# Attention layers, experts' selections and the x norm in a new order, and the mixer's output projection by token tiles

## The chip, the core and the metric

The kernel runs on one core of one Trainium2 chip. That core has a matrix engine (PE, TensorE), a vector engine (DVE), a scalar engine (ACT), GpSimd (POOL), a queue engine that issues the transfers (SP), and 16 DMA engines between memory and the on-chip buffer. Each engine runs its own list of instructions in order; they meet only at semaphores. The metric is the device time of one execution in microseconds (us), the median of several runs.

## What is computed

Two transformer blocks stand one behind the other on 256 tokens of width 1024, all in float32. The parts that matter here, cut from the reference:

```python
for i in range(DEPTH):                       # first_block: two layers
    h = rmsnorm(x, attn_norm[i]); proj = h @ w_in[i]
    ...                                      # dilated attention oa, windowed attention ob
    mix = jnp.concatenate([rmsnorm(merge_heads(oa), mix_norm_a[i]),
                           rmsnorm(merge_heads(ob), mix_norm_b[i])], axis=-1)
    x = x + mix @ w_out[i]
    ...                                      # layer 0: swiglu; layer 1: moe_swiglu, 8 experts, top 2
return rmsnorm(x, final_norm)

def ffn_half(s, shift, scale, gate, g_pre, g_post, w_in, w_out):      # second block
    h = swiglu_2(modulate(rmsnorm_2(s, g_pre), shift, scale), w_in, w_out)
    return s + 0.5 * gate * rmsnorm_2(h, g_post)
def token_mixer(...):
    ...
    return (g_hy * y_hy + g_da * y_da) @ w_o
```

The second block runs `ffn_half` on a context and on x, then the mixer (a long convolution and a differential attention), then another `ffn_half`.

## The kernel before

The tokens are two tiles (`tt`) of 128. A float32 operand of a large product is split into a high part (rounded to the fast format fp32r) and a low remainder, and a product is three matmuls, high by high, high by low and low by high. ACT makes every high part (a copy that rounds), DVE every low part (a subtraction); PE waits for both. A weight block is 1024 x 512 values and comes in two halves `h` of four 128-row chunks, so one half for one tile is 12 matmuls of 512 columns, and one block for one tile is two halves. `weight_high` and `weight_low` (L1588, L2255), or `A_parts` in the feed-forward phases (L1604, L2287), make the parts; the blocks lie in a ring of two (`ringA`), which SP refills as soon as a half has been used.

The order of work is written out by hand, engine by engine; no scheduler moves anything.

**Attention layers** (`heads` on PE, L1043, and its counterparts on ACT and DVE). 16 heads go through in four groups `g`. For each, PE turns the softmax weights (`turn_weights`, L1078), ACT copies heads 0 and 2 (L1890) and DVE heads 1 and 3 (L2620) back to memory, PE multiplies by the values (`values`, L1088 to L1090) and DVE normalises into `O` (`outputs`, L2625). Between these, PE works off rows of a modulation matrix (`mods`, L1038, `spreads`, L1020). The output goes through an rms norm in two halves: columns 0 to 511 (groups 0 and 1) and 512 to 1023 (groups 2 and 3). A half's norm is squares (`tile_stats`, L1565) and a square root (`tile_root`, L1569) on ACT, a scaling on DVE (`tile_scale`, L2236), transposes on PE (`turn_rows`, L736), a high part on ACT (`rows_high`, L1578) and a low part on DVE (`rows_low`, L2252). The first half's norm starts behind group 2. Then `project_split` (L763) multiplies by `w_out`: for block 0 tile 0 half 0, tile 0 half 1, tile 1 half 0, tile 1 half 1, and so on. Exponentials and square roots need different tables on ACT, so a table load stands at L1569.

**Experts.** Each of the eight experts works on at most 128 gathered tokens in 14 steps `n` (`expert`, L976 on PE, L1758 on ACT, L2408 on DVE). A step on PE is half a gate or up block (L903), two transposes (L918), the other half, and 12 matmuls of the down projection (L933), which wait for `hds`, the transposed activations split by ACT (L1704) and DVE (`part_low`, L2351). The result of expert e-1 is scattered behind steps 2 and 3 of expert e (L973), and DVE adds it to x (`add`, L2400). DVE also makes the selection matrices (`one_hot`, L2375): the gated one of e and the plain one of e+1, both behind step 3. Experts 1 to 6 are one hardware loop; inside an expert the first `head` pairs of steps are written out and the rest is a loop (`blocks`, L465).

**The norm of x behind the experts** stands within the first steps of the context's feed-forward phase `ff0c` (`x_rows`, L1972 on ACT, L2780 on DVE): the squares, a root, DVE's scaling by `final_norm`, squares and roots again (L1565), and another scaling (L2236). All of it stands in ACT's and DVE's lists ahead of `hidden` of step 1 (L1634, L2305), for which PE's down projection of step 0 waits (L858).

**The mixer's output projection `wo`** (L1303) is two blocks `n` for two tiles, eight half blocks. PE takes them as (n, h, tile) 000, 001, 010, 011, 100, 110, 101, 111. A tile is complete once both of its blocks are. Then come per tile the squares (L2151, L2159) and the root (L2160) on ACT, DVE's scaling and addition to x (`mixed_out`, `mixed_add`, L3021, L3026), and the norm for the last feed-forward phase `ff1` (L1565, L2236), which PE turns (L736) and multiplies (L806).

## Time and profile before

| | us |
|---|---|
| median of 3 runs | 2653.58 |
| the runs | 2653.3, 2653.58, 2659.06 |
| profiled execution, its own time | 2659.7 |
| its span, first to last instruction | 2657.9 |

PE is busy for 96% of the span, DVE for 68%, ACT for 55%; the mean granted clock of PE is 0.978 of full speed. A row of a timeline reads: start in us, duration in us, engine, line, operation, tile written and tiles read, shapes, number of instructions merged, and in brackets how long the engine sat idle before it and what ended that. "issue" stands there where the profile names no releaser.

### The profile page before, as it was taken

The page shows a single profiled execution, that of the slowest core. Times are in us where ns is not written, and L with a number is a line of the kernel's source. Part 1 is how long each engine was busy: PE and PEld are TensorE (multiplying, and loading weights), DVE is VectorE, ACT ScalarE, POOL GpSimd, SP SyncE. Part 2 cuts the span into 40 slices and gives each one's busy share as a digit, 9 for nine tenths or more (in the row PEclk, how much of TensorE's full clock was granted, in tenths as well). Part 3 has the DMA queues.
Part 4 walks back from the last instruction along what each step waited for, and adds up shares of the span by engine and source line. Part 5 has one row for each costly group of instructions (what it writes and reads, how often), then busy time and mean ns, then how long its engine had stood idle before and what let it go on. Part 6 is the DMA issues. An engine that isn't in the chain of part 4 may idle for free.

```text
span 2657.9 us, 33567 instructions
## 1 busy us (share of the span) xinstructions
PE 2548.6 (96%) x11951; PEld 2023.4 (76%) x11951; DVE 1814.3 (68%) x1779; ACT 1452.1 (55%) x1613; POOL 54.4 (2%) x40
## 2 busy tenths in 40 slices
PE   7899999889999999999999998999999999998998
PEld 6578887667878788888878786888884688776787
DVE  6464446558898888888888985645444475776544
ACT  4454444547777777776767774435432343465443
POOL 0000000010000000000000000500000000000000
PEclk9899999889999999999999999999999999998999
DMA  6865552659999999999999995755544244435551
GB/s 216 297 207 189 189 174 90 243 174 374 351 353 348 354 342 347 356 351 342 360 328 372 327 341 203 227 191 183 187 145 130 85 143 131 129 107 173 193 185 68
DMA packets 327743, 631.65 MB, mean 238 GB/s; under 512 B 14089, under 2 KB 112937, under 8 KB 327465
## 3 DMA queue, kind: packets, MB, share of 16 engines
q1 hardware_dynamic: 326792, 627.35, 68.0%
q0 software_dynamic: 864, 3.15, 0.4%
q8 instruction: 55, 0.90, 0.1%
q14 instruction: 32, 0.25, 0.0%
HBM read 629.40 MB, written 1.05 MB: 237 GB/s over the span
## 4 chain that ended last, share of the span: by engine, by line
PE 85%; DVE 7%; ACT 4%; issue 3%; DMA 1%; SPq 0%; DVEq 0%; ACTq 0%
PE ps L829 19%; PE ps L903 19%; PE ps L933 11%; PE ps L858 10%; PE ps L1303 6%; PE ps L763 5%; PE ps L1330 2%; PE ps L1235 1%; DVE As L2290 1%; PE ps L1038 1%; PE ps L958 1%; PE ps L918 1%; PE ps L842 1%; ACT Bs L1724 1%; ACT As L1694 1%
## 5 line engine op out<-in xcount | busy, mean ns | idle before, releaser
L2290 DVE TENSOR_TENSOR As<-ringA,As 128x2048 fp32r<-128x2048 f32 x318 | 730.9, 2300 | 227.4 <-ACT As L1613 131.9
L903 PE MATMUL ps<-As,xgs 128*128 128x512 f32 x2688 | 660.7, 395 | 5.7 <-DVE As L2290 3.0
L903 PEld LDWEIGHTS ps<-As,xgs 128*128 128x128 f32 x2688 | 494.8, 188 | 112.3 <-issue 5.8
L1694 ACT ACTIVATE As<-ringA 128x2048 fp32r<-128x2048 f32 x224 | 428.8, 1914 | 28.3 <-PE ps L903 28.1
L829 PE MATMUL ps<-As,xs 128*128 128x512 f32 x1456 | 376.1, 396 | 3.9 <-DVE hh L2325 3.9
L933 PE MATMUL ps<-Bs,hds 128*128 128x512 f32 x1332 | 322.4, 391 | 11.8 <-DVE hds L2351 9.0
L829 PEld LDWEIGHTS ps<-As,xs 128*128 128x128 f32 x1456 | 271.9, 189 | 63.3 <-DVE hh L2325 4.8
L933 PEld LDWEIGHTS ps<-Bs,hds 128*128 128x128 f32 x1332 | 248.6, 188 | 69.9 <-issue 16.5
L2370 DVE TENSOR_TENSOR Bs<-ringB,Bs 128x2048 fp32r<-128x2048 f32 x111 | 254.1, 2290 | 12.4 <-ACT Bs L1724 10.8
L858 PE MATMUL ps<-Bs,hds 128*128 128x512 f32 x1056 | 250.6, 393 | 4.1 <-issue 4.1
L1724 ACT ACTIVATE Bs<-ringB 128x2048 fp32r<-128x2048 f32 x111 | 213.1, 1920 | 69.4 <-PE ps L933 69.4
L858 PEld LDWEIGHTS ps<-Bs,hds 128*128 128x128 f32 x1056 | 199.9, 190 | 47.0 <-issue 4.5
L1613 ACT ACTIVATE As<-ringA 128x2048 fp32r<-128x2048 f32 x94 | 179.8, 1913 | 29.1 <-PE ps L829 12.8
L2334 DVE TENSOR_TENSOR Bs<-ringB,Bs 128x2048 fp32r<-128x2048 f32 x44 | 103.7, 2358 | 118.1 <-ACT Bs L1667 118.1
L1667 ACT ACTIVATE Bs<-ringB 128x2048 fp32r<-128x2048 f32 x44 | 84.3, 1915 | 136.5 <-PE ps L858 136.5
L2260 DVE TENSOR_TENSOR ringL<-ringA,ringH 128x2048 fp32r<-128x2048 f32 x42 | 96.1, 2290 | 56.5 <-ACT ringH L1593 56.3
L1704 ACT ACTIVATE hds<-ps 128x256 fp32r<-128x256 f32 x112 | 43.2, 385 | 153.9 <-PE ps L918 151.3
L763 PE MATMUL ps<-As,xs 128*128 128x512 f32 (+1 forms) x384 | 117.7, 390 | 7.8 <-DVE ringL L2260 5.7
L1634 ACT ACTIVATE hds<-ps 128x256 fp32r<-128x256 f32 x94 | 31.3, 382 | 169.8 <-PE ps L842 161.7
L1593 ACT ACTIVATE ringH<-ringA 128x2048 fp32r<-128x2048 f32 x42 | 80.2, 1911 | 79.2 <-PE ps L1303 57.6
L829 PE MATMUL ps<-As,xnR 128*128 128x512 f32 x352 | 112.8, 402 | 1.8 <-issue 1.8
L1655 ACT ACTIVATE sg<-ps 128x256 f32<-128x256 f32 x94 | 36.1, 385 | 125.9 <-PE ps L829 124.8
(390 smaller groups left out, 3300.3 us busy)
## 6 DMA issues: line engine op xcount, KB each, us to landing
ringA<-in_moe_w_gate SPq DMA_DIRECT2D x112, 1024.0 KB, 5.2
ringA<-in_moe_w_up SPq DMA_DIRECT2D x112, 1024.0 KB, 5.6
ringB<-in_moe_w_down SPq DMA_DIRECT2D x112, 1024.0 KB, 5.6
ringA<-in_w_ff_in SPq DMA_DIRECT2D x132, 512.0 KB, 4.7
ringA<-in_w_in SPq DMA_DIRECT2D x56, 1024.0 KB, 5.3
ringA<-in_w_ada SPq DMA_DIRECT2D x36, 1024.0 KB, 5.8
ringB<-in_w_ff_out SPq DMA_DIRECT2D x33, 1024.0 KB, 5.0
ringA<-in_dense_w_gate SPq DMA_DIRECT2D x28, 512.0 KB, 3.6
```

The costliest lines, as they stand in the source:

```text
L763: m = mm(ps[:, 4 + 2 * (n % 2) + tt, 0:cols], xs[:, l, k, tt * P:(tt + 1) * P], w, start=k == 0 and m_ == 0, stop=k == KC - 1 and m_ == 2)
L829: m = mm(ps[:, bank, :], lhs(l, tt, k), As[:, h, r, k % 4, :], start=k == 0 and n == 0, stop=k == KC - 1 and n == 2)
L858: m = mm(ps[:, 4 + 2 * tt + half, :], hds[:, buf, l, q, :], w[:, half * 512:(half + 1) * 512], start=first and q == 0 and n == 0, stop=q = ...
L903: m = mm(ps[:, bank, :], lhs(l, tt, k), As[:, h, r, k % 4, :], start=k == 0 and n == 0, stop=k == KC - 1 and n == 2)
L933: m = mm(ps[:, 4 + 2 * tt + half, :], hds[:, u if T == 1 else tt, l, q, :], (Bs[:, q, r, :] if weights is None else weights[r][:, q, :])[: ...
L1303: m = mm(dst, lhs[l][:, k, tt * P:(tt + 1) * P], w[q], start=k == 0 and m_ == 0, stop=k == KC - 1 and m_ == 2)
L1613: A(As[:, h, 0, :, :], ringA[:, (p["a"] + u) % 2, 4 * h:4 * h + 4, :], ACT.Copy).then_inc(A_high, 1)
L1694: A(As[:, h, 0, :, :], ringA[:, (p["a"] + u) % 2, 4 * h:4 * h + 4, :], ACT.Copy).then_inc(A_high, 1)
L1724: A(Bs[:, :, 0, :] if dst is None else dst, ringB[:, b0 % 2, :, :], ACT.Copy).then_inc(B_high, 1)
L2290: V.tensor_tensor(As[:, h, 1, :, :], ringA[:, (p["a"] + u) % 2, 4 * h:4 * h + 4, :], f32(As[:, h, 0, :, :]), ALU.subtract).then_inc(A_spli ...
L2334: V.tensor_tensor(Bs[:, :, 1, :], ringB[:, (p["b"] + u) % 2, :, :], f32(Bs[:, :, 0, :]), ALU.subtract).then_inc(B_low, 1)
L2370: V.tensor_tensor(lo, ringB[:, (p["b"] + u) % 2, :, :], f32(hi), ALU.subtract).then_inc(B_low, 1)
```

## The change

It reorders instructions; the arithmetic stays. In four places:

1. **Attention layers.** ACT takes the squares of the first half of the norm ahead of the last modulation row of group 2, loads the square root's table between its two copies of group 3, and takes the root behind them. DVE scales that half behind its copies of group 3 instead of behind group 2. PE takes `values(3)` and `mods(8)` ahead of the first half's transposes. ACT makes the high part of weight half 0 ahead of the squares of the second half, and that of half 1 behind the last `spreads`; DVE takes the low part of the first half's rows behind the scaling of the second.
2. **Experts**, on DVE alone: the second `add` moves behind `part_low` of step 4, the gated `one_hot` behind step 4 and the plain one behind step 5; three pairs of steps are written out instead of two.
3. **The x norm**: the second squares and roots, the table load and the second scaling move behind `hidden` of step 1, by a new hook `within`.
4. **`wo`**: the half blocks go 000, 001, 010, 100, 110, 011, 101, 111, so tile 0 is complete after five of them. ACT's statistics follow that order, and weight half 1 of `ff1` is split behind tile 0's rows instead of ahead. The added 1 in `TILES_THROUGH` makes SP's load of that half wait for the sixth half block, where it waited for the fourth.

```diff
+        TILES_THROUGH[ph["wo"]["a"]] += 1
...
                     if g == 3:
+                        values(g)
+                        mods(8)
                         pe.wait_ge(nm_ready, 4 * (l + 1))
                         for tt in range(TILES):
                             turn_rows(f"mix{l}", tt, 0)
-                        values(g)
-                        mods(8)
                         spreads(8)
                         continue
...
-            for n in range(2):
-                for h, tt in ((0, 0), (0, 1), (1, 0), (1, 1)) if n == 0 else ((0, 0), (1, 0), (0, 1), (1, 1)):
...
+            for n, h, tt in ((0, 0, 0), (0, 0, 1), (0, 1, 0), (1, 0, 0), (1, 1, 0), (0, 1, 1), (1, 0, 1), (1, 1, 1)):
+                if tt == 0:
...
                         before(2 * i + u)
                     if not (leads and isinstance(i, int) and i == 0 and u == 0):
                         hidden(*((i, 0) if u else (i - 1, 1)))
+                    if within and isinstance(i, int):
+                        within(2 * i + u)
...
                         if j == 0:
+                            if g == 3:
+                                nc.scalar.preload_act_table(ACT.Sqrt)
                             spreads(2 * g + 1)
+                    if g == 2:
+                        for tt in range(TILES):
+                            tile_stats(f"mix{l}", tt, O, [(o_done, 4 * l + 2)], slice(0, D // 2), tt)
                     if g < 3:
                         mods(2 * g + 2)
                         exponentials(g + 1, (0, 1))
                         spreads(2 * g + 2)
                         exponentials(g + 1, (2, 3))
                         mods(2 * g + 3)
-                    if g == 2:
-                        for tt in range(TILES):
-                            tile_stats(f"mix{l}", tt, O, [(o_done, 4 * l + 2)], slice(0, D // 2), tt)
-                        tile_root(0, 2, D // 2)
+                tile_root(0, 2, D // 2)
...
                 p = ph[f"out{l}"]
+                weight_high(p, 0, 0)
+                for tt in range(TILES):
+                    tile_stats(mix, tt, O, [(o_done, 4 * (l + 1))], slice(D // 2, D), 2 + tt)
+                mods(8)
+                tile_root(2, 4, D // 2)
                 for tt in range(TILES):
                     rows_high(mix, tt, 0, mixc)
-                for h in range(2):
-                    weight_high(p, 0, h)
-                mods(8)
-                for tt in range(TILES):
-                    tile_stats(mix, tt, O, [(o_done, 4 * (l + 1))], slice(D // 2, D), 2 + tt)
-                tile_root(2, 4, D // 2)
                 spreads(8)
+                weight_high(p, 0, 1)
                 for tt in range(TILES):
                     rows_high(mix, tt, 1, mixc)
...
                 if n == 1:
                     act.wait_ge(x_ready, XR["moe"])
                     squares(lambda tt: x[:, tt, :], 1, 1e-5, lambda tt, q: x_tok[:, tt, :])
-                    for tt in range(TILES):
-                        tile_stats("ff0x", tt, x, [(x_ready, XR["final"])])
-                        tile_root(tt, tt + 1, D, 1e-6)
-                    nc.scalar.preload_act_table(ACT.Silu)
 
+            def x_stats(n):
+
+                if n == 1:
+                    for tt in range(TILES):
+                        tile_stats("ff0x", tt, x, [(x_ready, XR["final"])])
+                        tile_root(tt, tt + 1, D, 1e-6)
+                    nc.scalar.preload_act_table(ACT.Silu)
+
...
-            for tt in range(TILES):
-                act.wait_ge(tile_done, p["td"] + tt + 1)
+            def mixed_first(tt):
+
+                act.wait_ge(tile_done, p["td"] + 2 * tt + 1)
...
-            for h in range(2):
-                A_parts(ph["ff1"], 0, 0, 0, h, fresh=True)
 
             def mixed_root(tt):
 
-                act.wait_ge(tile_done, p["td"] + 2 + tt + 1)
+                act.wait_ge(tile_done, p["td"] + 2 * tt + 2)
...
+            mixed_first(0)
+            A_parts(ph["ff1"], 0, 0, 0, 0, fresh=True)
             mixed_root(0)
+            mixed_first(1)
             tile_stats("ff1", 0, x, [(x_mixed, 1)])
             tile_root(0, 1, D, 1e-6)
             mixed_root(1)
             split_rows(0)
+            A_parts(ph["ff1"], 0, 0, 0, 1, fresh=True)
             tile_stats("ff1", 1, x, [(x_mixed, 2)])
             tile_root(1, 2, D, 1e-6)
             split_rows(1)
...
-                    if n in (2, 3) and not first:
-                        add(e - 1, n - 2)
-                    if n == 3:
+                    if n == 2 and not first:
+                        add(e - 1, 0)
+                    if n == 4:
                         if not first:
                             dve.wait_ge(selg_tp, e)
                         one_hot(e, 2 * e + 2, True)
-                        if not final:
-                            dve.wait_ge(gathered, 2 * e + 2)
-                            one_hot(e + 1, 2 * e + 3, False)
+                    if n == 5 and not final:
+                        dve.wait_ge(gathered, 2 * e + 2)
+                        one_hot(e + 1, 2 * e + 3, False)
...
                     if not lead:
                         part_low(e, i - 1, u, 1)
+                    if isinstance(i, int) and i == 2 and u == 0 and not first:
+                        add(e - 1, 1)
...
-                blocks(dve, NB1, body, 2)
+                blocks(dve, NB1, body, 3)
...
                     if g == 3:
                         for tt in range(TILES):
-                            rows_low(mix, tt, 0, mixc)
+                            tile_scale(mix, tt, O, 1, lower, tt)
                     outputs(g)
-                    if g == 2:
-                        for tt in range(TILES):
-                            tile_scale(mix, tt, O, 1, lower, tt)
                 weight_low(p, 0, 0)
                 for tt in range(TILES):
                     tile_scale(mix, tt, O, 2, upper, 2 + tt)
+                for tt in range(TILES):
+                    rows_low(mix, tt, 0, mixc)
                 weight_low(p, 0, 1)
                 for tt in range(TILES):
                     rows_low(mix, tt, 1, mixc)
...
                     last.then_inc(x_ready, 1)
-                    dve.wait_ge(x_ready, XR["final"])
-                    for tt in range(TILES):
-                        tile_scale("ff0x", tt, x, tt + 1)
+            def x_scale(n):
+
+                if n == 1:
+                    dve.wait_ge(x_ready, XR["final"])
+                    for tt in range(TILES):
+                        tile_scale("ff0x", tt, x, tt + 1)
+
...
             mixed_out(0)
             mixed_add(0)
-            A_parts(ph["ff1"], 0, 0, 0, 1)
             tile_scale("ff1", 0, x, 1)
             plain_rows(0)
             mixed_out(1)
             split_rows(0)
             mixed_add(1)
+            A_parts(ph["ff1"], 0, 0, 0, 1)
             tile_scale("ff1", 1, x, 2)
             plain_rows(1)
             split_rows(1)
```

DVE's feed has the same `within` hook behind its `hidden`.

What stands on **ACT at the end of the attention of layer 1**, from the squares of the norm's first half on. `arena` holds the softmax weights and `O`, `xn` the normed rows, `xs` the split rows, `As` the high part of the weights, `arow` a modulation row. Before:

```order
L1565 ACTIVATE xn,ss<-arena 128x512 [waits o_done]
L1565 ACTIVATE xn,ss<-arena 128x512 [waits o_done,act_step]
L1569 ACT_TABLE_LOAD
L1569 ACTIVATE std<-ss,small 128x2 [waits act_step]
L1890 ACTIVATE arena<-ps 128x384 [waits pt_done] x2
L1578 ACTIVATE xs<-ps,vcol 128x128 [waits pn_tp]
L1578 ACTIVATE xs<-ps,vcol 128x128 x3
L1578 ACTIVATE xs<-ps,vcol 128x128 [waits pn_tp]
L1578 ACTIVATE xs<-ps,vcol 128x128 x3
L1593 ACTIVATE As<-ringA 128x2048 [waits A_full00]
L1593 ACTIVATE As<-ringA 128x2048 [waits A_full01]
L1684 ACTIVATE arow<-ps 128x512 [waits spread,tile_done]
```

And now (the squares of the first half stand further up):

```order
L1892 ACTIVATE arena<-ps 128x384 [waits pt_done]
L1895 ACT_TABLE_LOAD
L1892 ACTIVATE arena<-ps 128x384 [waits pt_done]
L1569 ACTIVATE std<-ss,small 128x2
L1593 ACTIVATE As<-ringA 128x2048 [waits A_full00]
L1565 ACTIVATE xn,ss<-arena 128x512 [waits o_done]
L1565 ACTIVATE xn,ss<-arena 128x512 [waits o_done,act_step]
L1686 ACTIVATE arow<-ps 128x512 [waits spread,tile_done,act_step]
L1569 ACTIVATE std<-ss,small 128x2
L1578 ACTIVATE xs<-ps,vcol 128x128 [waits pn_tp]
L1578 ACTIVATE xs<-ps,vcol 128x128 x3
```

The first copy of group 3 no longer stands behind squares, table load and root, and the first half's rows stand behind the second half's squares.

**DVE in steps 3 and 4 of an expert of the loop**, from the low part of the down weights (`Bs`) of step 3 on; `hds` is what PE's down projection waits for. Before:

```order
L2370 TENSOR_TENSOR Bs<-ringB,Bs 128x2x1024 [waits B_high]
L2398 REGISTER_ALU
L2400 TENSOR_TENSOR x<-x,ps 128x1024 [waits mixed_back]
L2379 ISA [waits selg_tp,added]
L2379 COPY small<-slots 128x2
L2380 REGISTER_ALU
L2380 COPY small<-gates 128x2
L2381 REGISTER_ALU
L2384 TENSOR_SCALAR arena<-c,small 128x128 [waits col_ready]
L2384 TENSOR_SCALAR arena<-c,small 128x128
```

And now:

```order
L2384 TENSOR_TENSOR Bs<-ringB,Bs 128x2x1024 [waits B_high]
L2364 REGISTER_ALU
L2365 TENSOR_TENSOR hds<-ps,hds 128x256 [waits hd_high]
L2412 REGISTER_ALU
L2414 TENSOR_TENSOR x<-x,ps 128x1024 [waits mixed_back]
L2301 REGISTER_ALU [waits added]
L2302 TENSOR_TENSOR As<-ringA,As 128x2048 [waits A_high]
L2301 REGISTER_ALU
L2302 TENSOR_TENSOR As<-ringA,As 128x2048 [waits A_high]
L2382 REGISTER_ALU
L2384 TENSOR_TENSOR Bs<-ringB,Bs 128x2x1024 [waits B_high]
L2393 ISA [waits selg_tp]
```

`hds` of step 4 stands directly behind step 3, and the addition and the selections behind it.

**ACT behind `wo`**, from its first statistics on (`fnrow` takes squares nobody reads, `std` the root). Before:

```order
L2151 ACTIVATE fnrow,ss<-ps 128x512 [waits tile_done]
L2152 ACTIVATE std<-ss,small 128x1 [waits act_step]
L2151 ACTIVATE fnrow,ss<-ps 128x512 [waits tile_done,act_step]
L2152 ACTIVATE std<-ss,small 128x1 [waits act_step]
L1613 ACTIVATE As<-ringA 128x2048 [waits A_full00,act_step]
L1613 ACTIVATE As<-ringA 128x2048 [waits A_full01]
L2159 ACTIVATE fnrow,ss<-ps 128x512 [waits tile_done]
L2160 ACTIVATE std<-ss,std 128x1 [waits act_step]
```

And now:

```order
L2161 ACTIVATE fnrow,ss<-ps 128x512 [waits tile_done]
L2162 ACTIVATE std<-ss,small 128x1 [waits act_step]
L1613 ACTIVATE As<-ringA 128x2048 [waits A_full00,act_step]
L2167 ACTIVATE fnrow,ss<-ps 128x512 [waits tile_done]
L2168 ACTIVATE std<-ss,std 128x1 [waits act_step]
L2161 ACTIVATE fnrow,ss<-ps 128x512 [waits tile_done]
L2162 ACTIVATE std<-ss,small 128x1 [waits act_step]
```

Tile 0's root no longer stands behind tile 1's first squares and the second half of `As`.

## Rows read from the trace of the kernel before

**Rows 1.** Waits of PE: engine, line, releaser, us in total, times, longest.
```profile
PE ps L933 <- DVE hds L2351: 9.3, 16, 1.1
...
PE ps L1078 <- ACT arena L1890: 4.9, 3, 2.4
```

**Rows 2.** Busy time by stretch: window, length, PE, PEld, DVE, ACT, POOL, PEclk, DMA, GB/s.
```profile
147.50:157.00 9.50, 9.50 (x43) 7.71 (x42) 6.50 (x9) 3.54 (x2) 0.00 (x0) 1.00 0.08 19
...
521.50:528.40 6.90, 6.90 (x34) 6.79 (x32) 2.72 (x9) 5.75 (x10) 0.00 (x0) 0.50 0.00 0
```

**Rows 3.** Timeline of PE, end of the attention of layer 0, then of layer 1.
```profile
137.39 0.39 PE L1090 MATMUL ps<-arena 128*128 128x64 f32 x2
137.61 0.39 PE L1088 MATMUL ps<-arena 128*128 128x64 f32 x2
...
149.10 0.63 PE L763 MATMUL ps<-As,xs 128*128 128x512 f32 x2
...
519.11 0.87 PE L1078 MATMUL ps<-c,arena 128*128 128x128 f32 x3 [2.19 <-ACT arena L1890]
...
540.85 0.63 PE L763 MATMUL ps<-As,xs 128*128 128x512 f32 x2
```

**Rows 4.** Timelines of ACT and of DVE in layer 1, the same place.
```profile
517.00 1.28 ACT L1569 ACT_TABLE_LOAD   x1
518.29 0.30 ACT L1569 ACTIVATE std<-ss,small 128x2 f32<-128x2 f32 x1
...
522.65 2.18 ACT L1578 ACTIVATE xs<-ps,vcol 128x128 fp32r<-128x128 f32 x8 [2.14 <-PE ps L736]
524.67 3.76 ACT L1593 ACTIVATE As<-ringA 128x2048 fp32r<-128x2048 f32 x2
...
537.86 2.15 DVE L2252 SCALAR_TENSOR_TENSOR xs<-ps,vcol,xs 128x128 fp32r<-128x128 f32 x8
```

**Rows 5.** Timelines of PE and DVE in steps 3 and 4 of expert 1.
```profile
758.94 3.03 PE L933 MATMUL ps<-Bs,hds 128*128 128x512 f32 x12 [1.08 <-DVE hds L2351]
...
755.47 1.21 DVE L2400 TENSOR_TENSOR x<-x,ps 128x1024 f32<-128x1024 f32 x1
...
758.33 0.42 DVE L2351 TENSOR_TENSOR hds<-ps,hds 128x256 fp32r<-128x256 f32 x1
758.67 4.49 DVE L2290 TENSOR_TENSOR As<-ringA,As 128x2048 fp32r<-128x2048 f32 x2
```

**Rows 6.** Busy time by stretch (columns as in rows 2): experts 1 to 6.
```profile
700.00:1470.00 770.00, 760.92 (x3518) 622.98 (x3517) 679.63 (x488) 545.83 (x402) 0.00 (x0) 1.00 0.97 350
```

**Rows 7.** DMA queues within 842:1472, experts 2 to 6: packets, MB, share.
```profile
q1 hardware_dynamic: 92960, 220.21, 96.4%
```

**Rows 8.** Timelines of PE and DVE at the x norm, first steps of `ff0c`.
```profile
1639.94 8.46 PE L858 MATMUL ps<-Bs,hds 128*128 128x512 f32 x24 [4.07 <-issue]
1648.24 1.04 PE L736 MATMUL ps<-c,arena 128*128 128x128 f32 x8
...
1632.32 2.48 DVE L2786 SCALAR_TENSOR_TENSOR x<-x,rr,fnrow 128x1024 f32<-128x1024 f32 x2
...
1639.41 0.76 DVE L2305 TENSOR_TENSOR hds<-ps,hds 128x256 fp32r<-128x256 f32 x2 [0.74 <-ACT hds L1634]
1641.48 2.29 DVE L2290 TENSOR_TENSOR As<-ringA,As 128x2048 fp32r<-128x2048 f32 x1 [1.32 <-ACT As L1613]
```

**Rows 9.** Timelines of PE, ACT and DVE behind `wo`.
```profile
2451.88 1.97 PE L736 MATMUL ps<-c,xn 128*128 128x128 f32 x8 [3.11 <-DVE xn L2236]
2456.99 5.13 PE L806 MATMUL ps<-As,xs 128*128 128x512 f32 x12 [3.14 <-DVE xs L3042]
...
2465.99 5.78 PE L806 MATMUL ps<-As,xs 128*128 128x512 f32 x24 [0.22 <-DVE xs L3042]
...
2444.67 0.58 ACT L2159 ACTIVATE fnrow<-ps 128x512 f32<-128x512 f32 x1
...
2440.63 2.29 DVE L2290 TENSOR_TENSOR As<-ringA,As 128x2048 fp32r<-128x2048 f32 x1 [4.25 <-ACT As L1613]
```

More of the change, by code:

```diff
@@ L1461, in _ @@
             free, p = p["jd"], ph["wo"]
-            for n in range(2):
-                for h, tt in ((0, 0), (0, 1), (1, 0), (1, 1)) if n == 0 else ((0, 0), (1, 0), (0, 1), (1, 1)):
-                    if tt == 0:
-                        weights_split(p, n, h)
-                    if n == 0:
-                        pe.wait_ge(ot_lo, 4 + 2 * h + tt + 1)
-                    if h == 0:
-                        pe.wait_ge(pj_dve, free + 2 * n + tt + 1)
-                    m = products(p, n, h, ps[:, 4 + 2 * n + tt, :], tt, split_h)
-                    if h:
-                        m.then_inc(tile_done, 1)
-                    elif tt == TILES - 1:
-                        m.then_inc(A_lo_free, 1)
-                    if n == 0 and h == 0 and tt == 0:
-                        pe.wait_ge(y_mixed, 4)
-                        turn_out(YH, 4, 1)
+            for n, h, tt in ((0, 0, 0), (0, 0, 1), (0, 1, 0), (1, 0, 0), (1, 1, 0), (0, 1, 1), (1, 0, 1), (1, 1, 1)):
+                if tt == 0:
+                    weights_split(p, n, h)
+                if n == 0:
+                    pe.wait_ge(ot_lo, 4 + 2 * h + tt + 1)
+                if h == 0:
+                    pe.wait_ge(pj_dve, free + 2 * n + tt + 1)
+                m = products(p, n, h, ps[:, 4 + 2 * n + tt, :], tt, split_h)
+                if h:
+                    m.then_inc(tile_done, 1)
+                elif tt == TILES - 1:
+                    m.then_inc(A_lo_free, 1)
+                if n == 0 and h == 0 and tt == 0:
+                    pe.wait_ge(y_mixed, 4)
+                    turn_out(YH, 4, 1)
             for hf in range(2):
@@ L1623, in x_parts, with feed @@
                     A(xs[:, 0, 4 * h:4 * h + 4, :], src[:, 4 * h:4 * h + 4, :], ACT.Copy).then_inc(high, 1)
-            def feed(p, T, e=0, ahead=False, head=1, leads=True, drains=True, before=None, split_rows=None):
+            def feed(p, T, e=0, ahead=False, head=1, leads=True, drains=True, before=None, within=None, split_rows=None):
                 nb = p["nb"]
@@ L1999, in context_end @@
                     stats(call["mixc"], [(x_ready, XR["ff0c"])], lambda tt: cs[:, tt, :], eps=1e-6)
-            feed(ph["ff0c"], 2, ahead=True, head=2, drains=False, before=x_rows)
+            feed(ph["ff0c"], 2, ahead=True, head=2, drains=False, before=x_rows, within=x_stats)
             feed(ph["ff0x"], 2, head=2, leads=False, before=context_end)
@@ L2295, in x_parts, with feed @@
                     x_low(src, done, h, high, split)
-            def feed(p, T, e=0, ahead=False, head=1, leads=True, drains=True, after=None, split_rows=None, settles=True):
+            def feed(p, T, e=0, ahead=False, head=1, leads=True, drains=True, after=None, within=None, split_rows=None, settles=True):
                 nb = p["nb"]
@@ L2309, in body @@
                         hidden(*((i, 0) if u else (i - 1, 1)))
+                    if within and isinstance(i, int):
+                        within(2 * i + u)
                     nxt = (i + 1, 0) if u else (i, 1)
@@ L2808, in context_end @@
                     scaled("mixc", cs)
-            feed(ph["ff0c"], 2, ahead=True, head=2, drains=False, after=x_rows)
+            feed(ph["ff0c"], 2, ahead=True, head=2, drains=False, after=x_rows, within=x_scale)
             feed(ph["ff0x"], 2, head=2, leads=False, after=context_end)
```

## The prediction

> **What bounds the kernel now.** The page shows PE as the engine that is nearly always at work; in the six experts from 700 to 1470 us it is busy for 760.92 of 770 us [rows 6]. The time is PE's work plus the gaps in it, and this change touches no matmul, so I read first the list of what PE waited for and then, gap by gap, the timelines of PE and of the engine named. Three places stand out. PE waits 9.3 us in 16 pieces for the split `hds` of the experts, made by DVE, and 4.9 us in 3 pieces for ACT's copies of the turned softmax weights [rows 1]. At the end of layer 1 the second of three groups of turns starts 2.19 us late, because ACT loads a table (517.00) and takes a root ahead of its first copy [rows 3, 4]. Behind the experts PE stands still for 4.07 us and then runs 24 matmuls in 8.46 us [rows 8]; behind `wo` it stands still for 3.11 and 3.14 us [rows 9]. Not every wait leaves PE at the same speed: the stretch behind the late turns of layer 1 has a granted clock of 0.50, the lower of the two levels, 1.2 GHz, while in layer 0 the stretch from 147.50 on has 1.00, 2.4 GHz [rows 2].
>
> **Attention layers.** I count each up to the first matmul of the second half of `w_out` for tile 0, the 13th of the projection; it is the second of the row at 540.85, at 541.08, and in layer 0 at 149.33 [rows 3]. Behind it nothing changes its place. Layer 1, after the change: PE is free to turn at 519.11 - 2.19 = 516.92. ACT's first copy then takes half a us (519.11 less the root's end, 518.59, is 0.52) to 517.4, the load 1.28 to 518.7 [rows 4], the second copy to 519.2. The values that need it (10 or 11 pairs at 0.22 us as in layer 0 [rows 3]) take 2.4 us, to 521.6. Then comes what is now in a row: DVE's two `outputs` (0.8), ACT's squares of the second half (1.5), the modulation row (0.5) and root (0.3), all estimates by the like pieces in front of 517.00, and the first half's high and low rows, each eight in 2.2 [rows 4], of which tile 0's four are needed. The projection starts at about 527.1. Its 12 matmuls end at 529.9. Here the order brings a **new wait**: the second half's weight is split only behind the rows: 1.9 high (half of 3.76) [rows 4], 2.3 low (as in [rows 9]), and tile 0's second rows 1.1 (half of 2.15) [rows 4]. That makes the 13th matmul start at 532.35, after a wait of 2.4. Gain 541.08 - 532.35 = 8.7. Against it stands the clock: if the new wait leaves PE at the low level for its next eight matmuls, each costs 0.2 more, 1.7 together; I take 7.0. At worst, if the low level of this stretch stays whatever the waits, I put it at 3.4, since then mostly the waits go and PE's own work is the limit. The same chain laid on layer 0, whose PE was mostly fast already, gives 143.45 for 149.33: 5.9, less the same 1.7, so some 4.5 with the bounds 3 and 5.9.
>
> The median run was 6 us shorter than the profiled one. I assume that part of this is the long slow stretch of layer 1 [rows 2] and credit layer 1 with 5.3 rather than 7.0 against the median.
>
> As to the table load, the row is 517.00 plus 1.28, and the root starts at 518.29 [rows 4]: the load costs its own 1.28 us and nothing behind it. The Trainium skill, "ScalarE: Activation LUTs", section "What ACT_TABLE_LOAD costs", adds a drain of about 1.38 us to each switch, about 2.66 in all. By that rule the second copy would come 1.4 us later in each layer and the sum would be 2.8 smaller; the trace does not show the drain, so I leave it out.
>
> **Experts.** Before, DVE goes from the low part of the down weights straight to the addition (755.47), then the two selections, then `hds` (758.33), and PE waits 1.08 us for it at 758.94 [rows 5]. After, `hds` follows the weights at about 755.9, two us before PE is free at 757.86: that wait goes. It occurs once in each of experts 1 to 6 with about 1.07, in expert 0 with 0.55 and in expert 7 with 0.20, together 7.2. The rest of the 9.3 [rows 1] are waits of 0.2 to 0.3 in steps 0 and 2, which nothing moves. What is late next is DVE itself: the 1.21 of addition [rows 5] and 0.8 of the gated selection now stand ahead of the next `hds`. Worked forward (addition to 757.3, two `As` of 4.49 together which wait for ACT, to 762.7, `Bs` 2.3 to 765.2, selection to 765.95) this is ready about 0.45 before PE is free at 766.4; the step behind it, with the plain selection, keeps 0.55. Over the stretch DVE is busy 679.63 of 770 us [rows 6], so there is room on average. If both margins are overestimated by 0.5 us at each expert, some 3 of the 7.2 return: 4 to 8.3 is my range, the upper end being every piece of step 3 and 2 gone.
>
> **The x norm.** Now the second squares and roots, a table load and DVE's second scaling stand ahead of `hidden`, whose low part ends at 1640.1 [rows 8]; after, ACT's copy can start behind the first root, and DVE's `hds` stands directly behind its scaling, done at 1634.80 [rows 8], before PE ends the previous step at 1639.94 - 4.07 = 1635.87. The 4.07 goes, and the 24 matmuls should take 5.6 instead of 8.46, since they no longer follow a pause. PE is through them at 1641.5 and through the turns (1.04) at 1642.5. What is late next is the split of block 2: ACT's work adds up to the same, less the 0.55 of the copy that now goes first, so its low part at DVE, 1641.48 plus 2.29 [rows 8], ends at about 1643.2. Before, the gate matmuls followed the turns at 1649.03. Gain 5.8; bounds 3 (the 24 still slow) and 6.9.
>
> **`wo`.** PE ends `wo` at 2451.88 - 3.11 = 2448.77. Tile 0 was complete two half blocks before that and is now complete three before, 36 matmuls of 0.24 us, at 2440.15. Its last squares started at 2444.67, behind the second half of `As` [rows 9]. Now DVE limits: ACT makes the first half of `As` without tile 1's squares ahead of it, 1.0 sooner, so its low part, which followed ACT at 2440.63 for 2.29, ends at 2441.9. Scaling (1.6), addition (1.25), squares (1.25), root (0.3) and scaling (0.9), estimates by the instructions of like shape, end at 2447.1, before PE is done. So its 3.11 wait goes; the 3.14 behind the turns stays, since high and low rows are as long as before. The eight turns may take 1.04 as in [rows 8] instead of 1.97 [rows 9]. The feed starts at 2452.7 instead of 2456.99, and tile 1's, before at 2465.99 [rows 9], at 2461.6 or so. Gain 4.2, bounds 2.5 and 4.5. The second half of the weight, loaded two half blocks later, lands about 2448 and is split by 2455.4, about when it is needed; this is the thinnest cover of this part.
>
> **Sum.** Against the profiled run of 2659.7: 4.5 + 7.0 + 7.2 + 5.8 + 4.2 = 28.7, so 2631.0. Against the median of 2653.58, with 5.3 for layer 1: 27.0, so 2626.5.
>
> **Rivals.**
> (a) DVE becomes the bound in the experts and the waits return two steps later: then the change does not do there what it says. For it: margins of half a us, and more work in a row on an engine that is 88% busy [rows 6]. Against: the average room of 90 us. Gain 21, **2632.5**. Chance 0.14.
> (b) The lower clock level stays in the layers whatever the order, for PE is fully busy at 0.50 from 521.50 [rows 2]; the parts there give 4 together, perhaps one late load besides: **2634**. Chance 0.15.
> (c) The new wait costs only itself, and no low level follows: 3.4 to 5 more, **2622**. For it: 1.00 from 147.50 on in layer 0, where PE had waited shortly before [rows 2]. Chance 0.11.
> (d) Slower: the new wait of 2.4 us stands *inside* the projection, and PE falls to the low level there. If it stayed low for all 96 matmuls of each projection, it would cost 0.2 x 96 x 2 = 38 and give **2665**. It decides against the change only if the low level outlasts some 70 matmuls of each; rows 2 show a fall lasting in layer 1 and none in layer 0. Chance 0.04.
> (e) DVE's loop body in the experts grows by the written-out pair, from 122 to 141 instructions. In 630 us of five experts only the data queue appears [rows 7], no fetch of instructions, so I put no price on a jump back. With 15 us of DVE idle per expert (90 over 6) [rows 6] a stall of 1 us per jump would be hidden, and one of 3 us where DVE has half a us of room would cost 2.5 at 5 jumps, 12 in all: **2639**. Chance 0.02. The Trainium skill, "Runtime: NRT & Kernel Launch", section "Instruction fetch mechanics", says that a taken branch to a target outside the window held stalls for a fetch; a longer body would make that likelier. No row here shows such a stall.
>
> **How the numbers follow.** The forecast has 0.54; its own range is 2622 to 2631. (a), (b) and most of (c) lie within 2618 to 2637, which is what I give: the summed lower bounds (3, 3.4, 4, 3, 2.5, together 16) would give 2637.7, the upper ones (5.9, 8.7, 8.3, 6.9, 4.5, together 34) 2619. A measurement tells 0.2%, or 5.3 us, from no change. Faster by more than that are the forecast, (a), (b), (c) and (e), 0.96 together, less 0.02 for parts failing together: 0.94. Within it 0.02, slower (d) 0.04.
>
> **What would show it.** Right: no wait at the second turns of group 3, a wait of about 2.4 us at the 13th matmul of each projection; the wait for `hds` down from 9.3 us to about 2; no idle time ahead of the 24 matmuls of `ff0c` and 5.6 us for them; one wait of 3 us behind `wo` instead of two. Wrong: waits for `hds` at steps 5 and 6 of the experts (a), a clock of 0.50 through the projections (b, d), a late second half of `ff1`'s weights.

## The result, and the profile after

The changed kernel takes 2629.09 us (median of four executions, 2618.15 to 2629.64). The kernel before takes 2655.76 (median of four, 2653.3 to 2659.06). The ratio is 0.9887, with a 95% interval of 0.9868 to 0.9905. Beside other kernels it was timed once more, with six executions: 2628.49 us, ratio 0.9895 [0.9877, 0.9913]. The forecast was 2626.5 us, in a range of 2618 to 2637.

Page of the changed kernel, part 1, then waits of PE (engine, line, releaser, us in total, times, longest):

```profile
PE 2533.8 (96%) x11951; PEld 2014.9 (77%) x11951; DVE 1814.5 (69%) x1779; ACT 1450.9 (55%) x1613; POOL 51.7 (2%) x40
...
PE ps L764 <- DVE xs L2264: 5.7, 4, 2.0
...
PE ps L737 <- DVE xn L2248: 5.4, 4, 1.8
...
PE ps L934 <- DVE hds L2365: 2.2, 8, 0.3
...
PE ps L1021 <- ACT arow L1686: 1.9, 1, 1.9
```

PE still has nearly all the time. The wait for `hds` fell from 9.3 us in 16 pieces to 2.2 in 8, and that for ACT's copies of the turned weights, 4.9 us before, is down to almost nothing [rows 1]. Two waits are larger than before: L764 for `xs` (2.0 us before) and the one for `arow`.

**A ledger of the two traces.** Both kernels issue the same matmuls, so one can ask at each point by how much the new one is ahead of the old. I took the starts of PE's instructions in both profiled executions (2659.7 and 2628.7 us) and noted where that lead changes:

| stretch, in the time of the kernel before | lead before it | lead behind it | gained | forecast |
|---|---|---|---|---|
| 0 to 119, not touched by the change | 0 | 3.6 | 3.6 | 0 |
| layer 0, up to block 1 of its out projection | 3.6 | 9.9 | 6.3 | 4.5 |
| dense feed-forward and layer 1 to 508 | 9.9 | 7.4 | -2.5 | 0 |
| layer 1, up to the context's norm at 552 | 7.4 | 14.6 | 7.2 | 7.0 |
| experts, to 1611 | 14.6 | 22.0 | 7.4 | 7.2 |
| x norm, to 1655 | 22.0 | 27.0 | 5.0 | 5.8 |
| to `wo` | 27.0 | 28.0 | 1.0 | 0 |
| behind `wo`, to 2481 | 28.0 | 31.0 | 3.0 | 4.2 |

The parts that were changed give 28.9 us by this ledger, where 28.7 were forecast. That this agrees to 0.2 us is partly luck, since two of the parts gave more than forecast and two less. A second profiled execution of the changed kernel (2628.95 us, from its later timing) gained 4.8 us in layer 0 instead of 6.3, and the same 7.2 in layer 1. Besides, 3.6, -2.5 and 1.0 us arose where nothing was changed. There the same instructions run at another level of the clock, and this turned out to be the real subject.

**Layer 1**, timelines of PE and of ACT, changed kernel (start, us, engine, line, operation, tiles, shapes, count, idle before and its releaser):

```profile
508.29 3.17 PE L1079 MATMUL ps<-c,arena 128*128 128x128 f32 x12 [0.72 <-ACT small L1871]
...
519.82 0.47 PE L764 MATMUL ps<-As,xs 128*128 128x512 f32 x1 [0.47 <-DVE xs L2264]
...
524.78 0.47 PE L764 MATMUL ps<-As,xs 128*128 128x512 f32 x1 [1.96 <-DVE xs L2264]
525.10 0.50 PE L764 MATMUL ps<-ringL,xs 128*128 128x512 f32 x1
525.40 1.05 PE L764 MATMUL ps<-As,xs 128*128 128x512 f32 x2
...
509.23 0.49 ACT L1892 ACTIVATE arena<-ps 128x384 f32<-128x384 f32 x1 [0.99 <-PE ps L1079]
509.74 1.28 ACT L1895 ACT_TABLE_LOAD   x1
511.04 0.49 ACT L1892 ACTIVATE arena<-ps 128x384 f32<-128x384 f32 x1
```

The twelve turns run without a pause, where they had one of 2.19 us. The load takes 1.28 us and the copy follows 0.02 later, so there is no drain in this trace. The 13th matmul waits 1.96 us where 2.4 were forecast, and the next ones run at the low level: two in 1.05 instead of 0.63.

**Layer 0**, PE, then ACT:

```profile
131.96 1.21 PE L1021 MATMUL ps<-c,arow 128*128 128x2 f32 x8 [1.94 <-ACT arow L1686]
...
139.52 0.47 PE L764 MATMUL ps<-As,xs 128*128 128x512 f32 x1 [1.19 <-DVE xs L2264]
...
128.00 1.91 ACT L1593 ACTIVATE As<-ringA 128x2048 fp32r<-128x2048 f32 x1 [2.88 <-DMA ringA<-in_w_out]
129.82 0.61 ACT L1565 ACTIVATE xn<-arena 128x512 f32<-128x512 f32 x1
```

Here something happened that I had not seen. The high part of the weights now stands ahead of the squares, and it waits 2.88 us for `w_out` itself, which lands only at 128.0. The squares, the modulation row and the root queue behind it, and PE waits 1.94 us for the row. In layer 1 the weights lie ready and the same order costs nothing.

How much this costs differs from execution to execution. ACT waits for `w_out` in layer 0 in each of the nine traces with this order, for 0.6 to 2.9 us, and PE's wait for the row is 1.94, 1.9, 1.2, 0.8 and 0.8 us in five of them and none in the other four. In the second execution of the changed kernel it is none. There layer 0 follows the forecast chain, with the wait at the 13th matmul and the low level behind it, ACT first and then PE:

```profile
130.65 1.91 ACT L1593 ACTIVATE As<-ringA 128x2048 fp32r<-128x2048 f32 x1 [0.68 <-DMA ringA<-in_w_out]
...
142.54 0.47 PE L764 MATMUL ps<-As,xs 128*128 128x512 f32 x1 [1.92 <-DVE xs L2264]
...
144.04 1.05 PE L764 MATMUL ps<-As,xs 128*128 128x512 f32 x2
```

**x norm and `wo`**, PE:

```profile
1613.68 5.64 PE L859 MATMUL ps<-Bs,hds 128*128 128x512 f32 x24
1619.16 1.04 PE L737 MATMUL ps<-c,arena 128*128 128x128 f32 x8
1621.59 0.74 PE L830 MATMUL ps<-As,xnR 128*128 128x512 f32 x2 [1.39 <-DVE hh L2339]
...
2420.52 1.03 PE L737 MATMUL ps<-c,xn 128*128 128x128 f32 x8
2424.91 3.01 PE L807 MATMUL ps<-As,xs 128*128 128x512 f32 x12 [3.35 <-DVE xs L3061]
2429.74 1.88 PE L737 MATMUL ps<-c,xn 128*128 128x128 f32 x8 [1.83 <-DVE xn L2248]
```

The 24 matmuls have no pause ahead and take 5.64 us for 8.46 [rows 8]; 1.39 us come back at the next block. Behind `wo` the pause of 3.11 is gone and the second stays (3.14 before, 3.35 now) [rows 9], as forecast. But tile 1's turns, which had no pause before, now have one of 1.83. They run at the low level, 1.88 us for 1.03 before.

### The profile page after: what moved, and what is told of

It is laid out like the page before. It is cut to its first block, busy times and chain, and to the rows that moved or that the text cites. A ratio compares the mean times of both kernels' runs of the same rounds, so it can differ in the third digit from the quotient of the medians.

```text
span 2626.9 us, 33515 instructions
## 1 busy us (share of the span) xinstructions
PE 2533.8 (96%) x11951; PEld 2014.9 (77%) x11951; DVE 1814.5 (69%) x1779; ACT 1450.9 (55%) x1613; POOL 51.7 (2%) x40
## 3 DMA queue, kind: packets, MB, share of 16 engines
HBM read 629.40 MB, written 1.05 MB: 240 GB/s over the span
## 4 chain that ended last, share of the span: by engine, by line
PE 87%; DVE 6%; ACT 4%; issue 2%; DMA 1%; SPq 0%; DVEq 0%; ACTq 0%
PE ps L904 21%; PE ps L830 19%; PE ps L934 11%; PE ps L859 9%; PE ps L1304 6%; PE ps L764 5%; PE ps L1331 2%; PE ps L1236 2%; DVE As L2302 1%; PE ps L959 1%; PE ps L1039 1%; PE ps L919 1%; PE ps L843 1%; PE ps L1295 1%; ACT As L1696 1%
## 5 line engine op out<-in xcount | busy, mean ns | idle before, releaser
L764 PE MATMUL ps<-As,xs 128*128 128x512 f32 (+1 forms) x384 | 118.0, 390 | 11.3 <-DVE xs L2264 5.7
```

The source lines that it names most:

```text
L764: m = mm(ps[:, 4 + 2 * (n % 2) + tt, 0:cols], xs[:, l, k, tt * P:(tt + 1) * P], w, start=k == 0 and m_ == 0, stop=k == KC - 1 and m_ == 2)
```

## The experiments

### Each part alone

Each kernel is the one before with one of the four parts of the change, made by its pieces of the diff shown above.

> The kernel before with the new order of the two attention layers alone. Theory: the parts are independent, and this one gives 4.5 us in layer 0 and 5.3 to 7 in layer 1, so about 10 us (ratio 0.996); in the trace the second turn of group 3 does not wait, and the 13th matmul of each out projection waits about 2 us. Rival: the two compared profiles differed by 3.6 us at a point in layer 0 ahead of the change, so most of what layer 0 seems to give is the clock's chance; then this part gives 6 us or less. Second rival: the wait inside the projection leaves the matrix engine at the low level, and the part gives nothing.

> The kernel before with the new order of the additions and selections in the experts alone. Theory: the waits for hds (9.3 us in 16 pieces) fall to about 2.2 us, and the time from expert 0 to the end of expert 7 falls by 7 to 8 us (ratio 0.997). Rival: the vector engine is the bound, and the waits come back at steps 5 and 6; then it gives 1 to 2 us.

> The kernel before with the x norm behind the first hidden products alone. Theory: the pause of 4.07 us and the slow 24 matmuls (8.46 instead of 5.6 us) go, and the split of the next weight block gives a part back: 5 us (ratio 0.998). Rival: the low level comes at another place nearby, and it gives 3 us.

> The kernel before with the half blocks of the output projection by token tiles alone. Theory: the pause of 3.11 us behind the projection goes, that of 3.3 us stays, and a new one of 1.8 us stands ahead of tile 1's rows: 3 us in all (ratio 0.999). Rival: my sum of 4.2 us holds and the smaller number seen with all four parts comes from their meeting.

| part alone | us, median | ratio, 95% interval | executions | forecast for the part |
|---|---|---|---|---|
| attention layers | 2645.7 | 0.9955 [0.9939, 0.9971] | 5 | 9.8 us |
| experts | 2648.14 | 0.9965 [0.9951, 0.9979] | 7 | 7.2 |
| x norm | 2652.33 | 0.9978 [0.9966, 0.9990] | 10 | 5.8 |
| `wo` | 2656.77 | 1.0001 [0.9990, 1.0012] | 10 | 4.2 |

The kernel before stood at 2657.07 in 23 executions beside them. In us the ratios are 12, 9, 6 and 0, 27 together, each with 3 to 4 us of noise either way. Three parts gave what was forecast within that noise. The intervals leave out the rivals for the attention layers (6 us or less, or nothing) and for the experts (1 to 2 us), but not the 3 us of the rival for the x norm. `wo` gave nothing that could be timed: its interval allows a gain of 2.7 us at most, neither the 3 us of its theory nor the 4.2 of its rival. Yet its one trace shows the same 3 us as the ledger above: its first pause gone, `[3.35 <-DVE xs]` and `[1.85 <-DVE xn]` left, and the 12 matmuls in 2.99.

### What the clock does to the times

Each execution comes with its mean granted clock. Over the 46 executions of the kernel before that were timed beside the experiments, the time rises by 0.70 us for each us of (1 - clock) x time. What is left around that line scatters by only 0.9 us, where the times themselves reach from 2651 to 2663. So nearly all of the scatter goes with the clock. This allows a rough division of each gain: the mean time less 0.7 x (1 - clock) x time is the part with the clock taken out, and the rest is the clock's. It takes for granted that the slope found in one kernel holds in the others, and the means are good to about 1 us.

| kernel | mean clock | mean time, clock taken out | against before |
|---|---|---|---|
| before | 0.979 | 2617.5 | |
| attention layers alone | 0.9836 | 2613.9 | -3.6 |
| experts alone | 0.9791 | 2609.9 | -7.6 |
| x norm alone | 0.9800 | 2614.8 | -2.7 |
| `wo` alone | 0.9791 | 2617.8 | +0.3 |
| all four, first and second timing | 0.9875, 0.9857 | 2603.5, 2602.6 | -14.0, -14.9 |

With the clock taken out the parts add up: -13.6 against -14.0 and -14.9. The experts' gain is nearly all waiting, and the attention's is mostly clock: about 4 us of waiting and 8 of clock. The traces say where. Busy time by stretch, 28 us around the end of layer 1: window, length, PE, PEld, DVE, ACT, POOL, PEclk, DMA, GB/s. The first five are of kernels with the old order of the attention (before; experts, x norm and `wo` alone; and one from further below, with a longer written-out part):

```profile
512.00:540.00 28.00, 22.95 (x111) 18.13 (x111) 13.96 (x34) 19.23 (x52) 4.57 (x12) 0.57 0.41 149
...
512.00:540.00 28.00, 22.99 (x126) 17.32 (x119) 11.93 (x27) 17.41 (x49) 2.48 (x4) 0.62 0.44 146
...
508.00:536.00 28.00, 22.42 (x110) 17.24 (x110) 14.50 (x35) 19.57 (x51) 5.42 (x14) 0.63 0.40 145
...
512.00:540.00 28.00, 22.91 (x106) 17.93 (x106) 14.49 (x35) 19.23 (x49) 5.35 (x14) 0.57 0.39 143
...
508.00:536.00 28.00, 22.84 (x107) 17.91 (x107) 14.22 (x35) 19.23 (x51) 5.08 (x14) 0.57 0.40 147
```

And with the new order: attention alone, the changed kernel, and the changed kernel again:

```profile
500.00:528.00 28.00, 24.66 (x154) 18.13 (x153) 17.76 (x41) 23.75 (x59) 7.73 (x18) 0.87 0.46 162
...
500.00:528.00 28.00, 23.78 (x151) 17.55 (x152) 18.09 (x42) 23.38 (x59) 7.64 (x18) 0.89 0.47 169
...
504.00:532.00 28.00, 24.68 (x154) 18.21 (x153) 17.68 (x39) 23.62 (x59) 7.95 (x18) 0.87 0.46 158
```

All five old ones spend most of this stretch at the low level, 0.57 to 0.63 on average, and the three new ones do not. The six other kernels with the new order, all further below, have 0.76 to 0.94 over 28 us there. The 0.76 is that of the kernel with both selections behind step 4:

```profile
508.00:536.00 28.00, 24.82 (x130) 19.05 (x129) 17.91 (x36) 22.11 (x54) 9.34 (x18) 0.76 0.41 149
```

Layer 0 gains in the same way. One can add up (1 - granted clock) x 4 us over windows of 4 us. From 112 to 152 the five old traces have 6.8 to 8.6 us of it, and the seven new ones without the edit by halves 1.7 to 5.1. From 492 to 552, layer 1, they have 10.2 to 13.7 and 3.4 to 6.8. The means differ by 4.6 and 7.3 us, and 0.7 times their sum is 8.3 us. That is the clock's share of 8, found a second way.

I had taken the long slow stretch of [rows 2] for an accident of one execution. It belongs to the old order. The old order puts three pauses of 0.7 to 2.2 us close together there, and the new one runs the turns, values and modulation row in one piece. That it is the nearness of these pauses that keeps the clock low is my inference: no run moved one of them alone.

The two kernels timed beside each other for `wo` say no more than the part alone. The second is the changed kernel without it:

> The changed kernel once more, beside the next two, so that small differences can be read on one chip: ratio 0.989 to the kernel before, by the result on record. If the parts add up as timed alone (0.9955, 0.9965, 0.9978, 1.0001) it is 0.990.

> The changed kernel without the change to the output projection of the mixer: the other three parts alone. Theory from the traces: 3 us slower than the changed kernel. Rival from the timing of that part alone (1.0001): no difference, since in most executions the pauses before cost no more than those after.

They took 2628.49 (0.9895 [0.9877, 0.9913]) and 2633.82 (0.9923 [0.9898, 0.9948]). That looks like 5 us, but the six executions without the part fall into two heaps, three at 2626.6 to 2629.0 with a clock of 0.985 to 0.987 and three at 2638.7 to 2646.0 with 0.978 to 0.981. With the clock taken out the two kernels differ by 0.8 us, less than the executions of either scatter. Whether this part is worth 0 or 3 us stays open.

### The experts: which move counts, and how much room is left

Put back the addition:

```diff
-                    if isinstance(i, int) and i == 2 and u == 0 and not first:
-                        add(e - 1, 1)
...
-                    if n == 2 and not first:
-                        add(e - 1, 0)
+                    if n in (2, 3) and not first:
+                        add(e - 1, n - 2)
```

> The changed kernel, but in the experts the second addition stands behind step 3 again, as before; the selections keep their new places. Before, addition and selections together made hds 1.08 us late. The addition alone ends at about 756.7 in the time of the kernel before, hds at 757.1, and the matrix engine is free at 757.9: no wait returns, the period of an expert stays at the new value (about 125.2 us). Rival: the addition is what was late, and the wait returns with 0.3 us or more in each.

Put back the selections (`n == 4` and `n == 5` become `n == 3` for both):

> The changed kernel, but in the experts both selections stand behind step 3 again; the addition keeps its new place. By the same sum (selections 1.6 us, hds ready at 757.5 against 757.9) no wait returns either, with 0.4 us to spare, and the period of an expert stays. Rival: the spare 0.4 us is used up by the selections' own wait, and each expert is 0.2 to 0.5 us longer.

Both selections behind step 4:

```diff
-                    if n == 5 and not final:
-                        dve.wait_ge(gathered, 2 * e + 2)
-                        one_hot(e + 1, 2 * e + 3, False)
+                        if not final:
+                            dve.wait_ge(gathered, 2 * e + 2)
+                            one_hot(e + 1, 2 * e + 3, False)
```

> The changed kernel, but both selections stand behind step 4. This puts 0.8 us more ahead of the hds that I reckoned to be ready 0.45 us before it is needed. If that margin is right, 0.3 to 0.4 us of wait returns in each of seven experts, 2 to 3 us in all. Rival: the vector engine has more room there than I reckoned, and nothing returns.

The kernel before, with `blocks(dve, NB1, body, 3)` and nothing else:

> The kernel before, with three pairs of steps written out in the vector engine's experts instead of two, and no other change. If jumps back or the length of the loop cost anything, the period of an expert (126.3 us before) differs; I expect no difference above 0.05 us and the same waits for hds, 9.3 us.

The distance from one expert's scatter product to the next can be read to 0.05 us here, since in this stretch the granted clock is 1.00. So one execution of each is enough:

| kernel | period of an expert, us |
|---|---|
| before | 126.30 |
| before, three pairs written out | 126.27 |
| changed | 125.20 |
| changed, addition back | 125.20 |
| changed, selections back | 125.60 |
| changed, both selections behind step 4 | 125.81 |

The whole times of the last three were 2627.49, 2636.21 and 2642.66 us, and that of the kernel before with three pairs 2651.86, beside 2657.21 for the kernel before. Their clocks (0.987, 0.984, 0.983 and 0.981) differ too, and single executions of that kind can't tell a few us.

Waits of PE, with selections back, and then with both behind step 4:

```profile
PE ps L904 <- DVE As L2302: 5.1, 9, 1.6
PE ps L934 <- DVE hds L2365: 2.7, 9, 0.5
...
PE ps L934 <- DVE hds L2365: 6.3, 15, 0.6
```

Four things follow. Moving the selections is the whole gain; the addition may stand where it stood. Moving the addition alone gains only 0.70 of 1.10 us. The 0.4 us lost per expert is what the rival said, but by another wait: I had followed `hds` alone, which is nearly in time (2.7 us for 2.2), but the next `As` is late, and PE waits 5.1 us in 9 pieces for it, 3.0 in 3 before. With both selections behind step 4 the wait returns with 0.6 us in each of seven experts (6.3 against 2.2 us), where 0.3 to 0.4 were expected. The room there was only 0.2 of the selection's 0.8 us, and I had reckoned 0.45. And the written-out pair costs and gains nothing.

### Filling the new wait of the projection

For block 0 of both out projections, half 0 of tile 1 goes ahead of half 1 of tile 0:

```diff
-                    for tt in range(T):
...
-                        for h in range(2):
+                    outer = n == 0 and PN[nm]["mixed"]
+                    for tt, h in ((0, 0), (1, 0), (0, 1), (1, 1)) if outer else ((0, 0), (0, 1), (1, 0), (1, 1)):
```

> The changed kernel, with block 0 of both out projections taken by halves: half 0 for tile 0, half 0 for tile 1, then half 1 for both. Theory: the wait at the 13th matmul (1.2 us in layer 0, 2.0 in layer 1) exists only because nothing stands between; tile 1's 12 matmuls of 2.8 us cover it. The waits go, and with them the low level behind the one of layer 1 (1.5 us): 3 to 5 us faster than the changed kernel. Rival: the second half's rows of tile 0 are made later still or tile 0's end, now 12 matmuls later, holds up the norm behind it; then it is the same within 1 us.

The waits went. PE, layer 1, of this kernel, the first matmul of block 0 and that of block 1:

```profile
522.58 0.47 PE L764 MATMUL ps<-As,xs 128*128 128x512 f32 x1 [0.47 <-DVE xs L2265]
...
533.80 0.40 PE L764 MATMUL ps<-Bs,xs 128*128 128x512 f32 x1
```

Block 0 takes 11.2 us in both layers, where it took 13.3 in layer 0 and 15.0 in layer 1: 5.9 us less (7.5 less than in the second trace of the changed kernel, which has 14.9 and 15.0). And the kernel was not faster: 2628.9 us, 0.9895 [0.9878, 0.9911], by five executions. With the clock taken out it was, by 3.8 us, 2598.8 for 2602.6, but its clock was lower, 0.9836 for 0.9857 and 0.9875. In its trace a low stretch lies over the values and the modulation row of layer 1 (16 of them in 3.40 us for 1.92), well ahead of the edit, and another at 1972 that the changed kernel has not. Two theories were left: chance, or a price of the order. The last kernel has the same edit, and the experts' addition back in its old place, which had changed no period:

> The changed kernel with block 0 of the out projections taken by halves, as timed once already, and with the experts' additions back in their old place (which left the period of an expert at 125.2 us). Timed before, the halves took 5.8 us of waiting and slow matmuls out of the two projections and the kernel was not faster (2628.9 against 2628.5 us), since its mean granted clock was lower, 0.9836 against 0.9857 and 0.9875. If the lower clock was chance, this kernel runs at 0.986 to 0.987 and in 2623 to 2625 us. If it belongs to the order, it runs at 0.983 to 0.984 again and in 2628 to 2630 us.

It ran in **2619.97 us** (2616.4 to 2632.47, six executions), ratio 0.9869 [0.9849, 0.9889]. Five of the six have a clock of 0.987 to 0.990; the sixth, 2632.47 us, has 0.981. With the clock taken out it is 2597.4, next to 2598.8. The same window of layer 1, in the two kernels with the halves (first the slower):

```profile
504.00:532.00 28.00, 26.73 (x148) 21.07 (x147) 17.44 (x36) 22.36 (x55) 8.86 (x18) 0.82 0.51 176
...
500.00:528.00 28.00, 26.66 (x157) 21.43 (x157) 20.80 (x41) 22.12 (x54) 9.78 (x18) 0.94 0.53 189
```

That is below both forecasts, and it speaks for chance. So with the clock taken out the halves' 4 to 5 us show in two kernels, and the order by halves doesn't force the lower clock. What the lower clock belongs to isn't settled. The two kernels differ also in the addition's place, and they ran on two chips, though the kernel before had the same mean clock on both (0.979). The clock scatters between the executions of one kernel as well, from 0.982 to 0.988 for the changed kernel. This kernel is the fastest of the study. Against the changed one it is 8.5 us ahead by the medians, but those come from two chips. By the ratios, each to the kernel before on its own chip, it is 7 us, of which 4 to 5 stay with the clock taken out, and the intervals of the two ratios overlap a little.

## Why the prediction was right, point by point

- **The sum.** 28.7 us were forecast against the profiled execution; the changed places give 28.9, and the two executions differ by 31.0. Against the median, 2626.5 were forecast and 2629.09 measured. That both agree so well is partly luck: timed alone, by their medians, the attention layers and the experts gave more than forecast and `wo` nothing, and these errors cancel.
- **Experts.** Right in mechanism and size: 7.2 forecast, 7.4 by the ledger, 7.6 with the clock taken out. Rival (a) didn't occur, but it was nearer than I thought: the margin that held it off was 0.2 us and not 0.45. And of the two moves only that of the selections was needed.
- **Layer 1.** Right, link by link: 7.0 forecast and 7.2 found, the new wait at 1.96 for 2.4, the low level behind it at 1.5 for 1.7. The step that failed is the next one, "I assume that part of this is the long slow stretch of layer 1". The stretch is in all five traces with the old order, so there was no ground for crediting 5.3 for 7.0 against the median. The attention part gave 12 us for 9.8, a difference inside the noise of that timing. Rival (b) fell with it. The price of (d), the low level through the whole projection, was never paid: in layer 1 the low level lasts 3.4 us behind the wait.
- **Layer 0.** Right in size: 4.5 forecast; 6.3 by the ledger, of which 1.5 is a low stretch of the old execution in the modulation row of 123.84, and 4.8 in the second execution of the changed kernel. The second execution also follows the chain that I wrote down, with 1.92 for the wait and the low level behind it. The first doesn't. The wait for the weights from memory wasn't in the chain; there it cost 1.9 us ahead of the projection, with a low stretch behind, and the wait inside shrank to 1.19. What I had wrong of the kernel before is "whose PE was mostly fast already". From 147.50 on it is fast, and I had taken that stretch for (c) as well. But between 120 and 147.5 it is at the low level for some 13 us, behind pauses like those of layer 1, and the five old traces all have that.
- **x norm.** Mechanism right, 5.0 for 5.8. The term that was too small is the return: the gate matmuls start at 1621.59, which is 1643.6 in the old time, for 1643.2, and 0.4 more is lost in the next steps.
- **`wo`.** This term failed: 4.2 forecast, 3.0 in the traces, nothing that could be timed. I followed tile 0 and not tile 1. PE now comes to tile 1's turns before its rows are scaled, and the 1.83 us at 2429.74 are new. DVE makes the low part of the second half of `As` between tile 1's addition and its scaling, which accounts for about 0.7 of them, since the root is done at 2428.0 and the scaling starts at 2428.7. The rest is the chain of addition, squares and root. Of the two pauses of 3.1 us only 1.1 us are gone in sum. The rest of the traces' gain is mostly 12 matmuls at the high level, 3.01 for 5.13 us, which by the timing of the part alone isn't kept.
- **Written-out pair** (rival e): no price, 126.27 for 126.30 us. No run shows a stall at a jump.

## What to carry to other kernels

Follow every instruction that a move delays to its own reader: the selections' place decided the experts, while the addition's move freed `hds` and held up `As`, and a weight's high part ahead of the squares is free only where the weight has landed. Where one operand of a product is late, look for products that can do without it: half 0 of tile 1 covered the wait for half 1. Read a second trace of the same kernel before building on a single wait: in layer 0 the two traces of the changed kernel wait at different places. And before a few us are compared, set each execution's clock beside its time: here 0.70 us for each us of (1 - clock) x time explained all but 0.9 us of the scatter.

## What was unexpected of the hardware

The low level of PE's clock can outlast the pauses ahead of it by far. At the end of layer 1 before, behind three pauses that add up to 3.8 us, PE stood at 0.50 for 24 us; the window of 28 us around it has a mean of 0.57. Five kernels with the old order had 0.57 to 0.63 there, and nine with the new order 0.76 to 0.94. It costs more than the pauses themselves: of the attention part's 12 us about 8 are clock. And it doesn't follow from a pause alone. The pause of 1.9 to 2.0 us at the 13th matmul is followed by it in all seven traces that have it in layer 1, but only in four of five in layer 0: the kernel with both selections behind step 4 has a pause of 1.90 us there and none. The first 88 us of the kernel, which are the same instructions in all versions, took 88.9 us in one execution and 83.9 in another.
